# Even layer's two attentions as one loop of 32 head-pair steps, and an up stage with its products in banks

## The reference

```python
def conv_ffn(h, w_up, dw_w, dw_b, w_down):
    u = causal_dwconv(h @ w_up, dw_w) + dw_b
    a, v = jnp.split(u, 2, axis=-1)
    return (jax.nn.silu(a) * v) @ w_down
...
def dense_gqa_attention(q, k, v):            # A: 8 heads of 64, 2 key heads
    def block(qi):
        sc = jnp.einsum('bqkgd,bskd->bkgqs', qi, k).astype(jnp.float32) * scale
        p = jax.nn.softmax(sc, axis=-1).astype(v.dtype)
        return jnp.einsum('bkgqs,bskd->bqkgd', p, v)
...
def mla_attention(q_lat, q_rope, c_kv, k_rope, w_uv):   # B: 8 heads, 64 + 32 wide
...
    oa = oa * jax.nn.silu(ga)
...
    ob = mla_attention(q_lat, q_rope, ckv, k_rope, w_uv) * jax.nn.silu(gb)
    return jnp.concatenate([oa, ob], axis=-1) @ w_out
```

## Time and profile before

| | before |
|---|---|
| median of 3 runs | 1492.09 us (1490.01 to 1492.94) |
| the profiled execution | 1496.06 us |
| its span | 1494.2 us |
| TensorE matmul busy | 92% |
| VectorE / ScalarE / GpSimd busy | 59% / 27% / 44% |
| mean granted TensorE clock | 0.963 |
| up stage | about 460 to 698 us |
| down stage | about 709 to 840 us |
| even attention, both phases | about 960 to 1177 us |

### The profile page before, as it was taken

How to read it: one execution, slowest core, us unless ns; L and a number is a source line. 1 busy time by engine, 2 the same in 40 slices (tenths; PEclk the granted TensorE clock), 3 DMA queues, 4 the chain that set the end, 5 groups by cost and what they waited for, 6 DMA issues and landing times. The chain is left out here.

```text
span 1494.2 us, 19092 instructions
## 1 busy us (share of the span) xinstructions
PE 1380.0 (92%) x7038; PEld 1070.4 (72%) x7038; DVE 882.2 (59%) x1451; ACT 403.5 (27%) x891; POOL 661.4 (44%) x523
## 2 busy tenths in 40 slices
PE   5999789999999999997999699899999888999996
PEld 5788566678888888885787568666566676876675
DVE  4996766833556689999681653444455344136544
ACT  2001335523122212112110221144455312134420
POOL 4674412235676667777397436410000063642220
PEclk9999989999999999999899799999999998999998
DMA  5431101112343345555563312100000032320111
GB/s 201 141 99 57 43 15 38 35 44 85 97 160 124 99 159 189 190 193 155 184 204 91 120 57 85 57 29 15 15 1 1 20 94 62 95 61 29 43 43 57
DMA packets 37376, 130.21 MB, mean 87 GB/s; under 512 B 4400, under 2 KB 4656, under 8 KB 37040
## 3 DMA queue, kind: packets, MB, share of 16 engines
q1 hardware_dynamic: 27072, 94.16, 20.3%
q10 hardware_dynamic: 10224, 34.94, 6.7%
HBM read 126.98 MB, written 2.10 MB: 86 GB/s over the span
## 5 line engine op out<-in xcount | busy, mean ns | idle before, releaser
L933 POOL TENSOR_TENSOR wlo<-raw,whi 128x1024 fp32r<-128x1024 f32 x171 | 423.5, 2477 | 14.3
L929 POOL TENSOR_TENSOR whi<-raw,ones 128x2 fp32r<-128x2 f32 x171 | 52.6, 308 | 781.8 <-DMA raw<-in_w 781.8
L432 PE MATMUL bank<-ysplit,whi 128*128 128x512 f32 x960 | 297.4, 391 | 3.7 <-DVE ysplit L1927 3.7
L432 PE MATMUL bank<-hhi,whi 128*128 128x512 f32 x648 | 271.8, 420 | 10.7 <-DVE hlo L1440 7.0
L432 PE MATMUL bank<-hhi,wlo 128*128 128x512 f32 x648 | 258.9, 400 | 0.0
L432 PE MATMUL bank<-hlo,whi 128*128 128x512 f32 x648 | 258.6, 399 | 0.0
L432 PEld LDWEIGHTS bank<-ysplit,whi 128*128 128x128 f32 x960 | 180.6, 188 | 41.6 <-issue 4.1
L930 POOL TENSOR_SCALAR whi<-raw 128x1022 fp32r<-128x1022 f32 x171 | 191.3, 1119 | 0.0
L432 PE MATMUL bank<-ysplit,wlo 128*128 128x512 f32 x480 | 187.3, 390 | 0.0
L432 PEld LDWEIGHTS bank<-hhi,whi 128*128 128x128 f32 x648 | 125.3, 193 | 48.6 <-issue 12.8
L432 PEld LDWEIGHTS bank<-hhi,wlo 128*128 128x128 f32 x648 | 125.2, 193 | 28.0
(11 more groups left out here) (255 smaller groups left out, 1974.5 us busy)
## 6 DMA issues: line engine op xcount, KB each, us to landing
raw<-in_w SPq DMA_DIRECT2D x171, 512.0 KB, 3.6
arena<-in_ada ACTq DMA_DIRECT2D x48, 512.0 KB, 4.3
xbuf<-in_xT SPq DMA_DIRECT2D x8, 256.0 KB, 4.8
first<-in_w ACTq DMA_DIRECT2D x1, 2048.0 KB, 8.2
xbuf<-in_w ACTq DMA_DIRECT2D x1, 2048.0 KB, 8.6
xbuf<-in_xT ACTq DMA_DIRECT2D x8, 256.0 KB, 4.9
out_t<-xbuf SPq DMA_DIRECT2D x8, 256.0 KB, 2.2
first<-in_uq ACTq DMA_DIRECT2D x1, 768.0 KB, 8.0
```

The costliest lines, as they stand in the source:

```text
L432: m = mm(b[:, :], w[:, s, k * P:(k + 1) * P], x, start=(k == 0 and part == 0), stop=(k == DC - 1 and part == 2))
L929: g.tensor_tensor(whi[:, s, 0:2], raw[:, s, 0:2], ones[:, :], ALU.mult)
L933: g.tensor_tensor(wlo[:, s, :], raw[:, s, :], whi[:, s, :].bitcast(F32), ALU.subtract)\
```

## The change

**Up stage.** The pool is six banks (`UP`), and an `a` half's bank is kept until its pair is multiplied: tanh is written to the bank, and both passes of `ffn_mul` read it there. `cact` is copied once into banks 4 and 5; each ada unit becomes two passes of 512 columns, bank by SBUF, with two sets of sums (`modc`, `modp`) that are added in `modulation`. Ada units start at unit 4, so 40 run in the up stage, then one per unit. The high and low parts of the first eight results are made at units 20 to 34, every second. TensorE waits for ada unit 39 before the down stage, and the down blocks of a unit go through the banks in another order.

**Even layer.** The queries and the key of A are split into high and low parts in `qkr` ahead of the loop. One loop of 32 steps (pair of heads p, token tile) takes A (p below 4) and B. Each step makes the scores of both heads (fp32r on row halves in A, fp32 in B), transposes both, and multiplies with the values stationary, so that the output comes with channels on the partitions. A spread of 1/sum per pair (`ab_spread`) takes the place of `turn2`. Two of the four `ega` units and all `egb` units are filler in steps 0 to 11, four pieces a step. `PREP_V`, `PREP_K` and `PREP_Q` place B's preparations. There are four query and key buffers instead of two.

```diff
-VB_AT = 29
+PREP_V = (12, 13, 14, 15)
+PREP_K = {12: 0, 13: 1, 14: 2, 15: 3, 20: 4, 21: 5, 24: 6, 25: 7}
+PREP_Q = {12: 0, 13: 1, 16: 2, 17: 3, 20: 4, 21: 5, 24: 6, 25: 7}
+AB_FILL = [("ega", 2), ("ega", 3), ("egb", 0), ("egb", 1), ("egb", 2), ("egb", 3)]
...
-ADA_AT = 12
+ADA_AT = 4
+ADA_UP = 2 * FC - ADA_AT
+
+
+def fa_first(i):
+
+    return (i - 20) // 2 if 20 <= i < 36 and i % 2 == 0 else None
 
 
 def ada_late(i):
 
-    j = 2 * FC - ADA_AT + 2 * (i - DC)
-    return range(min(j, 6 * DC), min(j + 2, 6 * DC))
+    j = ADA_UP + i - DC
+    return range(j, j + 1) if j < 6 * DC else ()
 
...
+UP, CACT = (0, 1, 2, 3, 6, 7), (4, 5)
 N_FILL, N_S, N_O = (0,), (1, 2), (3, 6)
+AB_FILL_BANK, AB_S, AB_O = (0,), (1, 2), (3, 6)
...
+        abp = area(6 * T).rearrange("p (s h n) -> p s h n", s=3, h=2)
+        abt = area(4 * T).rearrange("p (s h n) -> p s h n", s=2, h=2)
...
+        QF = [h_use[:, 4 * T:5 * T], h_use[:, 5 * T:6 * T], arena[:, 8 * T:9 * T], arena[:, 9 * T:10 * T]]
+        KF = [h_use[:, 6 * T:7 * T], h_use[:, 7 * T:8 * T], cosA, sinA]
...
-                            inline=False)
+                            inline=False, pool=UP)
...
+            pe.wait_ge(*dve_did.at(("ada", ADA_UP - 1)))
...
-                for n in range(DC if i < LATE else 0):
+                for n in (2, 3, 6, 7, 4, 5, 1, 0) if i < LATE else ():
...
+            def ab_scores(s):
+                p, qt = ab_steps[s]
+                if p >= 4 and qt == 0:
+                    for half in range(2):
+                        pe.wait_ge(*dve_did.at(("QF", 2 * (p - 4) + half)))
+                banks = [bank.take(pe, AB_S, ("S", "AB", s, half)) for half in range(2)]
+                if p < 4:
+                    for part, (q, k) in enumerate(((p, 8), (4 + p, 8), (p, 9))):
+                        for half in range(2):
+                            rows = slice(64 * half, 64 * half + 64)
+                            m = mm(banks[half][:, :], qkr[rows, q, qt * P:(qt + 1) * P], qkr[rows, k, :],
+                                   start=(part == 0), stop=(part == 2))
+                else:
+                    for half in range(2):
+                        x = p % 2 * 2 + half
+                        m = mm(banks[half][:, :], QF[x][0:96, qt * P:(qt + 1) * P], KF[x][0:96, :], start=True, stop=True)
+                m.then_inc(*s_done.up(("AB", s)))
...
+            def ab_values(s):
+                p, qt = ab_steps[s]
+                pe.wait_ge(*ptc.at(("AB", s, 1)))
+                if qt == 0:
+                    bank.take(pe, AB_O, ("O", "AB", p))
+                b = bank.tiles[found[("bank", ("O", "AB", p))]]
+                for kt in range(TT):
+                    for half in range(2):
+                        v = ev[:, kt, half * HD:half * HD + HD] if p < 4 \
+                            else vB[:, kt, (2 * p - 8 + half) * HD:(2 * p - 7 + half) * HD]
+                        m = mm(b[64 * half:64 * half + 64, qt * P:(qt + 1) * P], v,
+                               abt[:, s % 2, half, kt * P:(kt + 1) * P], start=(kt == 0), stop=(kt == TT - 1),
+                               skip_group_check=True)
+                m.then_inc(*pv_done.up(("AB", s)))
...
+            pe.wait_ge(*dve_did.at("eklo"))
+            pe.wait_ge(*act_did.at(("ev", 0)))
+            n = len(ab_steps)
+            for i in range(n + 4):
+                if i < n:
+                    ab_scores(i)
+                if i in PREP_V:
+                    values_b(i - PREP_V[0])
+                if 2 <= i < n + 2:
+                    ab_turn(i - 2)
+                if i in PREP_K:
+                    key_prep(PREP_K[i])
+                if 3 <= i < n + 3:
+                    ab_values(i - 3)
+                if i >= 6 and (i - 6) % TT == 0:
+                    ab_spread((i - 6) // TT)
+                if i in PREP_Q:
+                    query_prep(PREP_Q[i])
+                if i < 2 * len(AB_FILL):
+                    if i % 2 == 0:
+                        part = unit(*AB_FILL[i // 2], inline=False, pool=AB_FILL_BANK)
+                    for k in range(4):
+                        part(i % 2 * 4 + k)
...
+            def ab_exp(s):
+                p, qt = ab_steps[s]
+                for half in range(2):
+                    x = n_col(p, half, qt)
+                    act.wait_ge(*sm_ready.at(("AB", s)))
+                    if s >= 3:
+                        act.wait_ge(*pt_done.at(("AB", s - 3, half)))
+                    A(abp[:, s % 3, half, :], bank.of(("S", "AB", s, half))[:, :], ACT.Exp, bias=nmax[:, x:x + 1],
+                      scale=ab_scale(p, half, qt), accum_out=rsum[:, x:x + 1]).then_inc(*p_ready.up(("AB", s, half)))
+                    bank.freed(("S", "AB", s, half), p_ready, ("AB", s, half))
...
-                V.tensor_tensor_reduce(ada[:, j % 2, :], ada[:, j % 2, :], cact, 1.0, 0.0, ALU.mult, ALU.add,
-                                       modc[:, j // (3 * DC), j % (3 * DC):j % (3 * DC) + 1])\
-                    .then_inc(*dve_did.up(("ada", j)))
+                if j >= ADA_UP:
+                    V.tensor_tensor_reduce(ada[:, j % 2, :], ada[:, j % 2, :], cact, 1.0, 0.0, ALU.mult, ALU.add,
+                                           modc[:, j // (3 * DC), j % (3 * DC):j % (3 * DC) + 1])\
+                        .then_inc(*dve_did.up(("ada", j)))
+                    return
+                for half, acc in enumerate((modc, modp)):
+                    at = slice(half * 512, half * 512 + 512)
+                    V.tensor_tensor_reduce(ada[:, j % 2, at], bank.tiles[CACT[half]][:, :], ada[:, j % 2, at], 1.0, 0.0,
+                                           ALU.mult, ALU.add, acc[:, j // (3 * DC), j % (3 * DC):j % (3 * DC) + 1])\
+                        .then_inc(*dve_did.up(("ada", j) if half else ("ada0", j)))
...
-                link(V.scalar_tensor_tensor(ft[:, j % 2, :], ft[:, j % 2, :], 1.0, ua[:, sa, :], ALU.add, ALU.mult))
-                V.tensor_tensor(fa[:, j, :], ft[:, j % 2, :], ua[:, sv, :], ALU.mult)\
-                    .then_inc(*dve_did.up(("fs", j)))
-
+                b, sa, sv = bank.of(("up", 2 * j)), (2 * j) % 4, (2 * j + 1) % 4
+                link(V.scalar_tensor_tensor(b[:, :], b[:, :], 1.0, ua[:, sa, :], ALU.add, ALU.mult))
+                V.tensor_tensor(fa[:, j, :], b[:, :], ua[:, sv, :], ALU.mult).then_inc(*dve_did.up(("fs", j)))
+                bank.freed(("up", 2 * j), dve_did, ("fs", j))
+
+            link(V.memset(modp[:, :, :], 0.0))
+            dve.wait_ge(*act_did.at("spread2"))
+            for half in range(2):
+                link(V.tensor_copy(bank.tiles[CACT[half]][:, :], cact[:, half * 512:half * 512 + 512]))
...
+            def q_low(c):
+                dve.wait_ge(*act_did.at(("eqhi", c)))
+                V.tensor_tensor(qkr[:, 4 + c, :], eq[:, c, :], qkr[:, c, :].bitcast(F32), ALU.subtract)\
+                    .then_inc(*dve_did.up(("eqlo", c)))
...
+            dve.wait_ge(*act_did.at("ekhi"))
+            V.tensor_tensor(qkr[:, 9, :], ek, qkr[:, 8, :].bitcast(F32), ALU.subtract).then_inc(*dve_did.up("eklo"))
+
+            def ab_max(s):
+                p, qt = ab_steps[s]
+                x = n_col(p, 0, qt)
+                dve.wait_ge(*s_done.at(("AB", s)))
+                for half in range(2):
+                    link(V.tensor_reduce(nmax[:, x + half:x + half + 1], bank.of(("S", "AB", s, half))[:, :], AX_X, ALU.max,
+                                         negate=True))
+                if p < 4:
+                    V.tensor_tensor(nmax[:, x:x + 2], nmax[:, x:x + 2], ab_scale(p, 0, qt, 2), ALU.mult)\
+                        .then_inc(*sm_ready.up(("AB", s)))
+                else:
+                    V.tensor_scalar(nmax[:, x:x + 2], nmax[:, x:x + 2], ab_scale(p, 0, qt), None, ALU.mult)\
+                        .then_inc(*sm_ready.up(("AB", s)))
...
+            def ab_out(p):
+                dve.wait_ge(*pe_did.at(("AB", "R", p)))
+                dve.wait_ge(*dve_did.at(("g", "ega", p) if p < 4 else ("g", "egb", p - 4)))
+                if p:
+                    dve.wait_ge(*dve_did.at(("AB", "y", p - 1)))
+                V.tensor_tensor(sgr, bank.of(("AB", "R", p))[:, :], esg[:, p, :], ALU.mult)\
+                    .then_inc(*dve_did.up(("AB", "sgr", p)))
+                bank.freed(("AB", "R", p), dve_did, ("AB", "sgr", p))
+                dve.wait_ge(*pv_done.at(("AB", p * TT + TT - 1)))
+                dve.wait_ge(*dve_did.at(("AB", "sgr", p)))
+                if p >= 2:
+                    dve.wait_ge(*dve_did.at(("ey", p - 2)))
+                V.tensor_tensor(sqt[:, p % 2, :], bank.of(("O", "AB", p))[:, :], sgr, ALU.mult)\
+                    .then_inc(*dve_did.up(("AB", "y", p)))
+                bank.freed(("O", "AB", p), dve_did, ("AB", "y", p))
```

419 lines of the change are left out of this document (146 added, 273 removed).

## The result

| | us | runs |
|---|---|---|
| before, median | 1492.51 (1490.01 to 1493.92) | 4 |
| changed, median | **1445.16** (1444.51 to 1450.07) | 4 |
| ratio | 0.9691, 95% interval 0.9669 to 0.9713 | |
| changed, the profiled execution | 1450.07 (span 1447.6) | the slowest of its four |

The change takes 47.3 us off. The forecast was 1432 with a range of 1415 to 1452: inside the range, but the gain is 12 us short of the 59.7 that I had summed.

A forecast was written before the change was run, and what follows sets the result against it. TensorE, busy 1380.0 of 1494.2 us, was taken as the bound. Up stage 12.7, key's spread to projection 45.4 and projection start 1.6 make 59.7 off 1496.06: 1436.4, less 4.0 for the median, 1432 us; range 1415 to 1452.

The forecast's parts named there:

- the wait of 3.4 for L1773: Ahead of the down stage: new TensorE wait for ada unit 39, 5 x 0.67 = 3.4 us.
- the debt: Up stage: VectorE falls behind TensorE, causing the 10.85 us wait at its end; claimed to go.
- the second wait and half of the slow clock: Down stage's start: the 3.40 us wait goes, and 1.9 of 3.6 us of slow clock is gained.
- prelude: Key's spread to first scores: spread, turn, one gate unit and a 4.9 us wait for the key's low part, 12.0 us.
- The bare steps: Ten phase B steps without preparation: scores wait for exp to free both banks, 5.2 us each instead of 3.55.
- The drain: Last scores to output projection: claimed 1.0 us shorter than a bare step.
- Clock in the bare steps: Phase B steps without preparation: idling causes a few clock drops, 4 us added.
- The first (smaller waits): Clock, down stage, prelude and bare steps: waits smaller than forecast, 14.5 us better, about 1418; chance 0.13.
- the second: Bare steps and after both waits: clock stays low, about 1450 us; chance 0.15.
- The third: Up stage: gives nothing, bank passes held up too or ada late, about 1445 us; 0.13 shared with the fifth.
- The fourth, slow pairs: Whole even-layer loop: half-array pairs too light, clock stays at 0.5, about 1534 us; chance 0.04.
- The fifth, no pairing: Phase A scores: halves run one after the other, 1.4 not 0.89 us, about 1440; 0.13 shared with the third.

The follow-up runs named there:

- e7: Changed kernel with the gate's product and ada both over SBUF again, earlier ada starts kept: 1457.47 us, ratio 0.9746.
- e2: Kernel before with only the even layer's part of the change, up stage as before: 1454.71 us, ratio 0.9728.
- e6: Changed kernel with the gate's product through SBUF again, ada still in banks: 1443.63 us, ratio 0.9664.
- e12: Changed kernel with phase B's key rope moved to step 3 and one copy in each of steps 12 to 15: 1445.35 us, ratio 0.9678.
- e8: e5 with only the value preparations two steps early, key and query preparations back in their old places: 1430.39 us, ratio 0.9574.
- e3: Changed kernel where each phase B half waits for its own bank and signals its own scores: 1435.00 us, ratio 0.9605.
- e9: Changed kernel with phase A's six score matmuls issued head after head instead of alternately: 1449.95 us, ratio 0.9702.
- e4: Changed kernel with ada as one 1024-column pass over SBUF again, product still in banks: 1445.95 us, ratio 0.9671.
- e10: Changed kernel with the sixteen value matmuls of every step issued head after head: 1454.09 us, ratio 0.9724.
- e5: e3 with a third gate unit ahead of the loop in bank 7 and preparations two steps earlier: 1427.54 us, ratio 0.9554.
- e11: e8 with phase B's key rope in step 3 and one copy in each of steps 10 to 13: 1423.67 us, ratio 0.9539.

## Why the prediction was right, and where it was off

**Up stage: right, mechanism and size.** Forecast 10.85 - 3.4 = 7.45 for the stage, found 7.5; the wait of 3.4 for L1773 is 3.33. e7 shows that the debt was VectorE's: with both passes over SBUF it returns. What I did not see is that one of the two edits is enough. (A small slip of the sum: four half ada passes are 4 x 0.68 = 2.7 us, not 3.0.) Behind it I forecast 5.3, the second wait and half of the slow clock, and found 3.6. The slow clock shrank from 17 to 3.4 us as hoped. Against it stand a second slow stretch of 3.4 us (807.8 to 811.2, clock 0.51, some 1.7 lost), behind a wait of 2.17 us for GpSimd's split of the down weights, and 0.7 us more of waiting in the norms. The wait for GpSimd is in the kernel before too (2.3 us), without a slow stretch behind it; so it is in e2 and e6, while the ten other kernels of the experiments have the drop. What decides that is open.

**Key's spread to projection: right in mechanism, 8.4 us short.** By the parts of the sum, from the starts of the steps:

| | forecast | measured | off |
|---|---|---|---|
| prelude, to the first scores | 12.0 | 12.7 | 0.7 |
| steps 0 to 11, with 2.5 of clock | 68.6 | 71.4 | 2.8 |
| steps 12 to 15 | 23.9 | 26.0 | 2.1 |
| steps 16 to the projection, with 4 of clock | 96.5 | 99.4 | 2.9 |
| sum | 201.0 | 209.4 | 8.4 |

- *The prelude.* The wait for the key's low part is 5.5 where I counted 4.9.
- *Steps 0 to 11.* The term "0.89 + 0.88 + 0.92 + 2.94" = 5.63 measured 5.89. Scores and filler are as priced; the eight transposes take 1.03 from their start to that of the values (1004.90 to 1005.93) instead of 2x0.44, since I had priced them from four alone, and the values 1.02 instead of 0.92 where filler follows. In steps 3 to 11 that makes 2.3 us. Another 0.9 is a wait for exp ahead of step 9 (991.33) that the sum did not have; the first three steps, with start-up and slow clock, came out 0.4 under. In a sum over hundreds of small groups, 0.1 us a group decides.
- *Steps 12 to 15.* I counted 0.6 for bank 0; the waits for it come to 2.0 (0.61, 0.53, 0.87), with 0.28 for exp besides, and VectorE "1.55 to 4.4" a step left out the key's rope and its copies, which held VectorE from 1015.0 to 1021.2 while the scores had ended at 1018.1. e12 puts 1.3 us on that, and e8 shows its full price, 5.18, once the step has no filler to cover it. This operation was in the code, in no row that I had read.
- *The bare steps.* "3.3 us before the next scores" is 3.53: the product 0.23 instead of 0.16, and exp hands over later (1116.17 to 1116.40). Ten steps at 5.5 instead of 5.2 cost 3. That the wait is the two-bank chain is shown by e3, which takes 1.5 us off a step without a spread and 0.8 off one with it, and leaves 0.7 us of waits.
- *The drain.* I made it 1.0 shorter than a bare step; from the last scores it took 13.4, where 9.7 stood in the sum: 2.1 are a wait for the first of the copies L1305, which stand behind both exps in ScalarE's order, and the rest is the slow clock at 1128 (e12's drain, with the same wait and no slow clock, takes 11.9).
- *Clock in the bare steps.* The 4 us for "a few drops" were not needed in this execution. That alone makes the other terms' misses look smaller, and it was luck of this execution: in kernels with the same steps 16 to 31, drops fell there in e12 and e2 (two each), e7 and e9 (one each) and e6 (three, where they cost 3.9 us); in e4 and e10 none did. In the four kernels where the waits for the banks are gone (e3, e5, e8, e11) none did either.

**SP and GpSimd** were costed at nothing, and no wait of TensorE in the stretch names them.

**Rivals.** The first (smaller waits) did not occur. Nor did the second as priced: the stretch 1060 to 1120 reads 1.00. The Trainium skill's rule ("TensorE: Matmul & The Clock Gate", section "A second HAM failure mode: psum-queue depth-cycling") was weighed for it; here one bank wait of 1.7 in 5.5 us did not make the clock swing as it says, though the single drops of 3.4 us named above (five of eight kernels with these waits, none of four without) are of its kind. That they come from the bank waits would fit and is, with so few executions, not shown. The third fell with L1806 and L1773 at 0.69 and 0.68. The fourth, slow pairs, fell: the clock is 1.00 in phase A from 946 us on. (Its price was wrong too: 169 us times 0.43/0.225 are 323, not 290, so it would have been at about 1567.) The fifth, no pairing, fell too, six scores take 0.89 us to the next start as in row 218.67, though e9 shows that the alternation is not needed for it. The projection's first matmul came 45 us earlier than 1180, not 57.

## What to carry to other kernels

When a loop waits for "both buffers", give each its own wait and its own signal before adding buffers or work: here it was worth 10 us for a few lines. Before counting cover, list everything that each engine issues in the step, the rare operations too: one 7.5 us job in a single step cost 1.3 us while other work stood there (e12) and 5 us once the filler was moved (e8). And when two edits pay off the same debt, try one: the second may be free of effect. The order of matmuls on the two halves of the array mattered where a half had eight of them, and not where it had three.

## What the runs showed of the hardware that I had not expected

- How long a VectorE pass over two SBUF tensors takes beside GpSimd's splits follows from when the GpSimd instruction ends. In e8 the rope's second and third pass (998.08 and 999.46, shown above) end at 999.43 and 1002.20, each some 0.54 us after the GpSimd instruction that was running when it started:

```profile
997.84 1.05 POOL L951 TENSOR_SCALAR whi<-raw 128x1022 fp32r<-128x1022 f32 x1
998.97 2.68 POOL L954 TENSOR_TENSOR wlo<-raw,whi 128x1024 fp32r<-128x1024 f32 x1
```

  The pass behind them (1002.23), with GpSimd idle, takes 0.68. The six product passes L1807 of e6 between 620 and 690 us (1.90 to 2.59 us) and the five L1786 of the kernel before between 620 and 670 us (1.92 to 2.29 us) also end 0.55 us after the GpSimd instruction, and the product's second pass, which starts in the gap that this leaves, takes 0.69. So such a pass looks held until GpSimd's instruction is done. The scale, product and ada passes of 512 columns with one operand in a bank stay at 0.68 to 0.70 on average in every kernel here.
- Six row-halved fp32r score matmuls take 0.97 us whether the halves alternate or not; sixteen column-halved value matmuls take 1.09 alternating and 1.58 not. The records of e9 and e10 show the second half starting ahead of two or three matmuls of the first.
- Slow stretches came after every wait of TensorE of 5 us or more in the even layer and went with it (e5, e8 and e11 have none at the prelude, all others have 6.8 us); after 3.3 us at the down stage's start one came in seven of ten executions, and in e3, e10 and e12 not.
